# Attention heads of the first block: the sums of squares are issued ahead of turns 0 and 1 on TensorE

## The reference, cut to what matters

```
q = rope(rmsnorm(q, q_norm_gain)); k = rope(rmsnorm(k, k_norm_gain))     # over the head dimension, 64
s = einsum('bqhcd,bkhcd->bhcqk', qblk, k) * scale                        # c = 0, 1; four blocks of 128 queries
p = softmax(where(mask, s, neg)); a = p[:, :, 0] - lam * p[:, :, 1]
o = einsum('bhqk,bkhe->bqhe', a, v)
o = rmsnorm(o, subln_gain) * (1.0 - lam_init)
```

## Time and profile before

| | us |
|---|---|
| median of 3 runs | 1397.55 (1394.72 to 1398.27) |
| the profiled execution | 1397.37 |
| its span | 1395.5 |
| TensorE busy | 1371.6 (98%) |
| VectorE busy | 685.8 (49%) |
| ScalarE busy | 832.2 (60%) |
| POOL busy | 204.9 (15%) |

### The profile page before, as it was taken

One profiled execution on the slowest core, in us unless ns is written; L12 is line 12 of the kernel. 1 busy time (PEld: TensorE's weight loads), 2 busy tenths in 40 slices (PEclk: granted clock), 3 DMA queues, 4 the chain that ended last, 5 costly groups with the idle time before them and its releaser, 6 DMA issues.

```text
span 1395.5 us, 18289 instructions
## 1 busy us (share of the span) xinstructions
PE 1371.6 (98%) x6634; PEld 1111.3 (80%) x6634; DVE 685.8 (49%) x1317; ACT 832.2 (60%) x1211; POOL 204.9 (15%) x240
## 2 busy tenths in 40 slices
PE   7999999999999999999999999999999999999998
PEld 5888777777788888888888887777798888888887
DVE  6993378988743455554145154745255201213324
ACT  7554777777665656665356366765667654535443
POOL 1111110110111111111111111100111111111112
PEclk9999999999999999999999999999999999999999
DMA  9998676576579888898987887755668798987973
GB/s 299 200 195 209 164 180 161 136 165 145 125 201 223 193 188 193 190 204 180 220 178 188 190 194 186 152 142 117 150 167 194 181 211 182 196 201 179 209 166 91
DMA packets 85670, 252.67 MB, mean 181 GB/s; under 512 B 16720, under 2 KB 24016, under 8 KB 85584
## 3 DMA queue, kind: packets, MB, share of 16 engines
q0 software_dynamic: 32400, 116.93, 46.4%
q1 hardware_dynamic: 51344, 131.06, 31.7%
q10 hardware_dynamic: 1840, 3.54, 0.7%
HBM read 126.98 MB, written 3.41 MB: 93 GB/s over the span
## 4 chain that ended last, share of the span: by engine, by line
PE 90%; DVE 5%; ACT 2%; DMA 2%; issue 1%; DVEq 0%; ACTq 0%
PE pg L646 26%; PE pg L648 25%; PE pg L647 25%; PE py L920 1%; PE ps L840 1%; DMA w_lo<-w_raw 1%; PE ps L815 1%; PE ps L816 1%; PE ps L817 1%; PE ps L1105 1%; PE ps L1113 1%; DMA act_lo<-w_raw 1%; DVE pairs L1842 1%; PE py L1123 1%; DVE acc L1845 0%
## 5 line engine op out<-in xcount | busy, mean ns | idle before, releaser
L646 PE MATMUL pg<-x_hi,w_hi 128*128 128x512 f32 x1008 | 397.5, 394 | 1.3 <-DVE gates L1842 1.3
L648 PE MATMUL pg<-x_hi,w_lo 128*128 128x512 f32 x1008 | 392.6, 390 | 0.0
L647 PE MATMUL pg<-x_lo,w_hi 128*128 128x512 f32 x1008 | 392.4, 389 | 0.0
L604 POOL DMA_DIRECT2D w_lo<-w_raw x221 | 190.4, 862 | 1149.1 <-ACT w_lo L1236 1074.0
L1235 ACT ACTIVATE w_hi<-w_raw 128x1024 fp32r<-128x1024 f32 (+1 forms) x215 | 224.4, 1044 | 116.9 <-PE pg L648 92.6
L646 PEld LDWEIGHTS pg<-x_hi,w_hi 128*128 128x128 f32 x1008 | 189.2, 188 | 50.3 <-issue 11.9
L1236 ACT ACTIVATE w_lo<-w_raw 128x1024 fp32r<-128x1024 f32 (+1 forms) x215 | 223.2, 1038 | 0.0
L648 PEld LDWEIGHTS pg<-x_hi,w_lo 128*128 128x128 f32 x1008 | 189.2, 188 | 39.9
L647 PEld LDWEIGHTS pg<-x_lo,w_hi 128*128 128x128 f32 x1008 | 189.3, 188 | 39.2 <-issue 1.0
L646 PE MATMUL pg<-act_hi,w_hi 128*128 128x512 f32 x424 | 165.1, 389 | 0.0
L647 PE MATMUL pg<-act_lo,w_hi 128*128 128x512 f32 x424 | 164.9, 389 | 0.0
(11 more groups left out here) (457 smaller groups left out, 1925.8 us busy)
## 6 DMA issues: line engine op xcount, KB each, us to landing
w_raw<-weights SPq DMA_DIRECT2D x218, 512.0 KB, 4.6
w_lo<-w_raw POOLq DMA_DIRECT2D x213, 512.0 KB, 5.6
kq_rot<-kq_raw SPq DMA_DIRECT2D x64, 64.0 KB, 2.2
w_raw<-weights SPq DMA_DIRECT2D x8, 384.0 KB, 3.7
w_lo<-w_raw POOLq DMA_DIRECT2D x8, 384.0 KB, 4.4
hid<-x SPq DMA_DIRECT2D x4, 512.0 KB, 5.4
hid<-x ACTq DMA_DIRECT2D x8, 256.0 KB, 5.4
act_lo<-w_raw POOLq DMA_DIRECT2D x4, 512.0 KB, 7.2
```

The lines of the kernel that those rows point to most:

```text
L604: pool.dma_start(low_of(u)[:, 0:n], w_raw[:, s, 0:n], accum_op=ALU.add).then_inc(lo_in[s], 16)
L646: pe.matmul(bank[:], wh, xh(k), start=n == 0, stop=False)
L647: pe.matmul(bank[:], wh, xl(k), start=False, stop=False)
L648: last = pe.matmul(bank[:], wl, xh(k), start=False, stop=n == len(ks) - 1)
```

## The change

The block of turns 0 and 1 moves behind the sums of k and of the output. Nothing else is changed; the order in which each PSUM bank is used stays as it is, since turns use `ps` and the sums `px` and `py`.

```diff
                     named(("gate", GATES_LAST[4]), XH, XL)
-                if attends:
-                    turn(g, 0)
-                    turn(g, 1)
                 if h < HEADS:
                     kq_sums(h, "k", 0)
                 if 2 <= h <= HEADS:
                     o_sums(h - 2)
+                if attends:
+                    turn(g, 0)
+                    turn(g, 1)
                 if attends:
                     scores(g, 2)
                     scores(g, 3)
```

## The result

The changed kernel takes 1401.34 us (median of 8 runs, 1400.11 to 1402.43) against 1397.2 us for the kernel before (8 runs beside them). The ratio is 1.0032, 95% interval 1.0022 to 1.0042, which is 3.1 to 5.9 us slower. The profiled execution took 1400.76 us.

What follows compares the result with a forecast made beforehand. In passes 2 to 4 a chain bounds the kernel: turn, ScalarE's copy and q, VectorE, the k tile's bank. 0.46 + 2.76 + 1.35 + 0.28 = 4.85 us on 1397.37 gave 1402.3 us, range 1398.8 to 1404.8.

Steps and rivals of the forecast that it cites:

- The sums find their operands ready: On TensorE behind the q tile: the moved sums' inputs are written in time, 0.7 us to spare, so no wait.
- Passes 2 to 4, the full 0.92 us each: VectorE's unbroken chain ends 0.92 us later and delays the k tile's first product on TensorE as much; 2.76 us.
- Pass 1: Ends in the same wait at the k tile, but only k's sums are moved there; 0.46 us.
- Passes 5 to 7, 0.45 us each, with about half swallowed: The next head's scores wait for VectorE's late `qq`; slack swallows the other half of 0.92 us; 1.35 us in all.
- TensorE's own wait, 0.23 to 0.32, taken as 0.28: Scores of block 2 wait uncovered for ScalarE's copy of turn 0, whose bank they write; 0.28 us.
- The 0.09 us gap: Time ahead of block 2's scores on TensorE even before the change; coming after the wait, it makes 0.32 of 0.23 us.
- pass 8: No k follows and VectorE has idle time at the end, so only TensorE's own wait counts; 0.28 us.
- The signs in the trace: Expected: turns 0.92 us later, about 0.2 us idle before block 2's scores, periods 25.6 (passes 2 to 4), 24.5 (5 to 7).
- The waits at the k tile: TensorE's wait for VectorE's `gates` product: about 0.83 us in pass 1, 0.85 in passes 2 to 4, against 0.65 and 0.21.
- A: Rival: only TensorE's own wait counts, VectorE's lateness is taken up on its way; 2.2 us, 1399.6; chance 0.14.
- B: Rival: passes 5 to 7 and 8 pay in full as well; 6.4 us, 1403.8; chance 0.12.
- C: Rival: not slower, since sums directly behind the q tile save 0.09 us a pass; 0.7 us gained, 1396.8; chance 0.10.

Runs made afterwards that it cites:

- The exchange on ScalarE: The changed kernel with ScalarE evacuating q ahead of its copy of turn 0 in all passes; 1.0013 against the kernel before, 1398.27 us.
- the two halves: Two runs: the kernel before with only k's sums, or only the output's, moved ahead of turns 0 and 1; each 1.0011, 1397.35 and 1397.39 us.

## Why the prediction was right

The forecast was +4.85 us, 1402.3; measured are +4.1 us by the medians (3.1 to 5.9), 1401.34, and +4.70 us in the heads' stretch.

- *The sums find their operands ready.* Right: the rows of TensorE after show them at a pitch of 0.23 us directly behind the q tile, and no wait of a sum is in its list.
- *Passes 2 to 4, the full 0.92 us each.* Right: the periods grew by 0.97, 0.92 and 0.98. Pass 1: forecast 0.46, measured 0.44 (22.77 against 22.33). The exchange on ScalarE shows the path, and the two halves show that it has no slack at all there: 0.46 us of lateness gives 0.45 to 0.52 us of period.
- *Passes 5 to 7, 0.45 us each, with about half swallowed.* Right: 0.43, 0.44, 0.41, with the wait for `qq` that was named. The halves show the slack: 0.46 us of lateness gives nothing.
- *TensorE's own wait, 0.23 to 0.32, taken as 0.28.* A little too large: the scores come 0.64 - 0.42 = 0.22 us late behind the turns (0.20 by the starts from the end of the q tile), and where nothing else stands beside it the period grew by 0.18. The 0.09 us gap does not come on top of the wait, so of the two sizes weighed, 0.23 fits. The reason given for it, weights that are already in place when the copy ends, is not what the records show: the first weight load of the scores starts with them (218.45; before 219.11), while that of a sum starts 0.23 us ahead of its matmul (218.56 for 218.79, before). Why the gap does not add is open. In pass 8 the forecast was 0.28; from that head's scores to the end of the stretch it grew by 0.11 (32.66 us before, 32.77 after), the one term that was clearly too large. Its scores 2 come 0.15 us later behind scores 0 (9.70 us against 9.55), 0.22 of wait less 0.07 us that scores 0 give back (see the last section).
- *The signs in the trace.* The idle time of about 0.2 us on TensorE ahead of the scores is not listed as such; it shows in the starts, as above. The waits at the k tile were forecast as 0.83 and 0.85 us and are 0.93 and 0.94, since TensorE loses less ahead of them than I took off; the periods of 25.6 and 24.5 came as written.
- *The rivals.* A (own wait alone, 2.2 us) falls with the passes 1 to 4 alone, +3.05 us in the stretch. B (the full price in passes 5 to 7) falls with their periods. C (no loss) falls with the interval.

The errors are small and of both signs: passes 2 to 4 together 2.87 us against 2.76, passes 5 to 7 1.28 against 1.35, pass 8 0.11 against 0.28. What remains between 4.70 in the stretch and 4.1 in the medians lies within the interval. The two profiles differ by 0.13 us behind the stretch, so nothing there speaks for a second effect.

Why a size of mine was off in the run with the late turns and the early gates product: there is a third wait in passes 2 to 5 of the kernel before that I had not seen. The q tile takes the bank that VectorE's other gates product frees. TensorE in pass 3, the product with the values (eight matmuls from 234.54) and then the q tile:

```profile
234.54 2.42 PE L920 MATMUL py<-pt,gates 128*128 128x512 f32 x8
...
236.91 0.47 PE L646 MATMUL pg<-x_hi,w_hi 128*128 128x512 f32 x1
```

VectorE at the same place:

```profile
236.07 0.69 DVE L1842 TENSOR_TENSOR gates<-pg,gates 128x512 f32<-128x512 f32 x1
```

The tile starts 0.15 us after that product ends, the same distance as at the k tile (227.09 to 227.23), and 2.37 us after the values, where pass 6 has 2.17 (308.17 to 310.34). No idle time is listed, because the last matmul of the values is still in progress in the records. The change moves both sides alike (2.36 us after), so it did not touch the forecast; where the gates product moves ahead and VectorE no longer waits for turn 3 (its copy, L2146), the distance is 2.18 (232.39 to 234.57 in the kernel before with that edit; 235.51 to 237.69 in the changed one), and the gain is larger than I worked out. With ScalarE's exchange as well VectorE still waits 0.45 us there, and the distance stays 2.36 (233.60 to 235.96), which is part of why that kernel's periods are 24.40 and not 24.31. In the changed kernel with that edit the scores also come 0.85 us ahead of the values (234.66 to 235.51) in place of 0.92 (233.70 to 234.62). Together that is 0.25 us in each of passes 2 to 5, 1.0 us in all, enough for the 0.7 us. No run takes the bank's wait away alone.

## What to carry to other kernels

Work that stands between a producer and a reader on the busiest engine is cover; before moving it ahead, list what waits for the producer on each other engine, and follow the lateness through their lists until a wait that is soft. Look above all for an instruction that is queued behind the late one without needing it: here that was the evacuation of q, and it carried two thirds of the loss. When two waits follow each other on an engine (0.84 for the turn, then 0.65 for q), ending the first one earlier can move its time into the second (1.59 us there); find the arm that ends last before paying for the other.

## What the runs showed that I had not expected

- A wait of 0.2 us on TensorE can be absent from its idle times when matmuls overlap (durations of 0.39 us at a pitch of 0.23). It shows in the pitch between starts (2.37 against 2.17 us, 1.55 against 1.35). The row of the weight loads can name what was waited for, but its idle time is not the wait: 0.39 us with one, 0.36 without.
- Scores that have waited for `qq` cost less afterwards: from the scores' first start to the values' it is 0.85 us (309.65 to 310.50) against 0.93 without a wait (307.24 to 308.17), so part of a wait at this place comes back.
- The time ahead of the heads varies by 3.3 us between profiles (183.61 to 186.88), more than most effects here; only the periods within the heads, which repeat within 0.1 us where the program is the same, could tell the parts apart.
